# Attention probabilities copied by DMA and transposed in one pass between the score products

## What is computed

```python
def sliding_window_attention(q, k, v, q_norm_g, k_norm_g, sinks):
    # 16 query heads in 4 groups of 4, one key/value head per group, head width 64, blocks of 128 tokens
    def block(args):
        qn, kn, vn, n = args          # keys: 16 meta tokens, the block before, the own block
        scores = einsum('bqhgd,bkhd->bhgqk', qn, keys) - slopes * dist
        scores = where(valid, scores, -inf)
        m = maximum(max(scores), sink)
        p = exp(scores - m)
        probs = p / (sum(p) + exp(sink - m))
        return einsum('bhgqk,bkhd->bqhgd', probs, vals)
```

## Time and profile before

| | |
|---|---|
| time, median of three runs | 1619.56 us (1619.38 to 1620.76) |
| span of the profiled execution, first to last instruction | 1618.2 us |
| TensorE busy | 1610.1 us, 99% |
| VectorE, ScalarE, GpSimd busy | 64%, 48%, 27% |
| granted TensorE clock | 1.000 over the span |

### The profile page before, as it was taken

How to read it: one execution, slowest core, us unless ns; L and a number is a source line. 1 busy time by engine, 2 the same in 40 slices (tenths; PEclk the granted TensorE clock), 3 DMA queues, 4 the chain that set the end, 5 groups by cost and what they waited for, 6 DMA issues and landing times.

```text
span 1618.2 us, 22594 instructions
## 1 busy us (share of the span) xinstructions
PE 1610.1 (99%) x7984; PEld 1347.5 (83%) x7984; DVE 1030.6 (64%) x1913; ACT 769.9 (48%) x1567; POOL 437.1 (27%) x675
## 2 busy tenths in 40 slices
PE   9999999999999999999999999999999999999999
PEld 6888888888888888888888888888888888888887
DVE  6775556655657676757565338866665657766675
ACT  6533334545547676763222126655545544444442
POOL 1101010221359888875221000121111122100000
PEclk9999999999999999999999999999999999999999
DMA  8323232645424343438553223344444399733452
GB/s 289 116 98 117 95 124 72 232 166 186 162 88 114 84 94 83 106 82 262 164 202 104 72 65 124 129 170 150 149 144 148 119 321 356 239 98 98 149 183 92
DMA packets 119599, 236.53 MB, mean 146 GB/s; under 512 B 13904, under 2 KB 48128, under 8 KB 119488
## 3 DMA queue, kind: packets, MB, share of 16 engines
q0 software_dynamic: 45904, 126.93, 23.6%
q1 hardware_dynamic: 73440, 108.03, 21.6%
q10 hardware_dynamic: 144, 0.13, 0.0%
HBM read 157.05 MB, written 69.47 MB: 140 GB/s over the span
## 4 chain that ended last, share of the span: by engine, by line
PE 97%; DVE 1%; DMA 1%; ACT 0%; SPq 0%; POOL 0%; issue 0%; DVEq 0%; ACTq 0%
PE bank L1084 29%; PE bank L1089 29%; PE bank L1088 29%; PE bank L1370 2%; PE bank L1402 2%; PE bank L1384 2%; PE bank L1419 0%; PE bank L1127 0%; PE bank L1502 0%; PE bank L1288 0%; PE bank L1406 0%; PE bank L1452 0%; DMA PX<-in_w_in 0%; PE bank L1387 0%; DVE WL L2172 0%; PE bank L1427 0%
## 5 line engine op out<-in xcount | busy, mean ns | idle before, releaser
L1084 PE MATMUL bank<-WH,ADH 128*128 128x512 f32 x448 | 174.3, 389 | 0.0
L1088 PE MATMUL bank<-WH,ADL 128*128 128x512 f32 x448 | 174.3, 389 | 0.0
L1089 PE MATMUL bank<-WL,ADH 128*128 128x512 f32 x448 | 174.3, 389 | 0.0
L1084 PE MATMUL bank<-HN,WH 128*128 128x512 f32 x384 | 152.4, 397 | 0.0
L2098 ACT CAST ADH<-ARAW 128x512 fp32r<-128x512 f32 x112 | 69.5, 621 | 169.9 <-PE bank L1089 160.9
L1089 PE MATMUL bank<-HN,WH 128*128 128x512 f32 x384 | 150.3, 391 | 0.0
L1088 PE MATMUL bank<-HN,WL 128*128 128x512 f32 x384 | 150.0, 391 | 0.0
L959 POOL TENSOR_SCALAR PR<-PR,RC 128x272 f32<-128x272 f32 (+1 forms) x128 | 131.0, 1099 | 44.9 <-DVE RC L2663 44.4
L2917 DVE TENSOR_TENSOR ADL<-ARAW,ADH 128x512 fp32r<-128x512 f32 x112 | 77.5, 692 | 96.9 <-ACT ADH L2098 96.7
L1084 PE MATMUL bank<-SOPH,WH 128*128 128x512 f32 x256 | 99.8, 390 | 0.0
L1089 PE MATMUL bank<-SOPL,WH 128*128 128x512 f32 x256 | 99.6, 389 | 0.0
(11 more groups left out here) (356 smaller groups left out, 4242.8 us busy)
## 6 DMA issues: line engine op xcount, KB each, us to landing
ARAW<-uop SPq DMA_DIRECT2D x112, 256.0 KB, 3.0
uop<-US POOLq DMA_DIRECT2D x64, 256.0 KB, 2.8
WRAW<-in_w_up SPq DMA_DIRECT2D x15, 1024.0 KB, 6.2
RAW<-in_w_in SPq DMA_DIRECT2D x58, 256.0 KB, 4.0
gates<-TB POOLq DMA_DIRECT2D x48, 256.0 KB, 2.4
uop<-UA POOLq DMA_DIRECT2D x48, 256.0 KB, 3.1
proj<-SA POOLq DMA_DIRECT2D x36, 256.0 KB, 2.5
RT<-proj POOLq DMA_DIRECT2D x8, 1024.0 KB, 8.8
```

Source lines behind the costliest of these rows:

```text
L1084: mm = pe.matmul(bank, ahi, bhi, start=first, stop=False, skip_group_check=onto)
L1088: pe.matmul(bank, alo, bhi, start=False, stop=False, skip_group_check=onto)
L1089: return pe.matmul(bank, ahi, blo, start=False, stop=last, skip_group_check=onto)
```

## The change

The probabilities of a pair are copied by a DMA of SyncE's queue from `PR` (fp32) into a new tile `PW` of two slots, whose type is fp32r, and TensorE transposes them from there with the fp32r identity `IDR`, one pass each. The transposes belong to pair T-3 instead of T-2 (LAG = 3), so that the loop has 68 steps and all that follows the transposes (`take_p`, `lo_p`, `values`, the moves of outputs) comes one step later; `values` stand in odd steps now. The transposes are no longer one group ahead of the query and key transposes: they stand singly behind the score products. To make room for `PW`, the keys and values of the blocks (`KV`) lie in a ring of four (NKV) instead of eight places, with their loads on GpSimd moved to steps 20, 28, 36 and 44, and the two weight blocks that lay in free places of it have a place of their own (`RAWA`). `PR` is freed for the next scores by the copy's landing, not by the transposes. As 220 gate steps are now spread over 68 steps, `new_slabs` gives 2, 3, 3 blocks in steps 6 to 8, 3, 3, 2 in steps 26 to 28, and 4, 3, 1 in steps 46 to 48.

```diff
@@ constants
-STEPS = NPAIR + 3
+LAG = 3
+STEPS = NPAIR + LAG + 1
-KV_FREE = {4: (6, 7), 5: (0, 7), 6: (0, 1)}
+ASIDE = (4, 5, 6)
+
+NKV = 4
@@ sync: the loop
+            def copy_p(pair):
+
+                n, b = pair // 8, pair % 2
+                lo, hi = (0, 2 * NKEY) if n else (P, P + 2 * NKEY0)
+                sp.wait_ge(pn_rdy, pair + 1)
+                if pair >= 2:
+                    sp.wait_ge(pt_full, pair - 1)
+                sp.dma_start(PW[:, b, lo:hi].bitcast(F32), PR[:, pair % 3, 1 + lo:1 + hi]).then_inc(pw_full[b], 16)
+
             for T in range(STEPS):
+                if 2 <= T < NPAIR + 2:
+                    copy_p(T - 2)
...
-                if T >= 4 and T % 2 == 0:
-                    G = (T - 4) // 2
+                if T >= LAG + 2 and T % 2 == 1:
+                    G = (T - LAG - 2) // 2
@@ tensor: the loop
-            def transpose_p(pair):
-                n, b = pair // 8, pair % 3
-                pe.wait_ge(pn_rdy, pair + 1)
-                if pair >= 1:
-                    pe.wait_ge(pl_rdy, split_of(pair - 1))
...
+            def transpose_p(pair, c):
+                n, b = pair // 8, pair % 2
+                if c == 0:
+                    pe.wait_ge(pw_full[b], PW0 + 16 * (pair // 2 + 1))
+                    if pair >= 1:
+                        pe.wait_ge(pl_rdy, split_of(pair - 1))
...
+                elif c // 2 in slots_of(n):
+                    key = pr_slot(n, c % 2, c // 2) - 1
+                    pe.transpose(B[4][:, c * P:(c + 1) * P].bitcast(F32R), PW[:, b, key:key + P], IDR[:, :])
...
-                if T < NPAIR:
-                    scores(T)
+                for i in range(5):
+                    if T < NPAIR and i < 4:
+                        score(T, i)
+                    if LAG <= T < NPAIR + LAG:
+                        transpose_p(T - LAG, i)
@@ vector: top(T)
                 if T >= 3:
-                    dve.wait_ge(pt_full, T - 2)
+                    dve.wait_ge(pw_full[(T - 3) % 2], PW0 + 16 * ((T - 3) // 2 + 1))
```

More of the change, by code:

```diff
@@ L589, in raw_block @@
                 return RAW[:, place, :] if place < 4 else RAWE[place - 4][:, :]
-            if k in (4, 5) and slab in KV_FREE:
-                return KV[:, KV_FREE[slab][k - 4], :]
+            if k in (4, 5) and slab in ASIDE:
+                return RAWA[:, k - 4, :]
             return RAWE[k - 4][:, :] if k >= 4 and slab == SLAB_E and RA_E else RAW[:, raw_slot(slab, k), :]
@@ L1358, in _, with score @@
                     ahead[i]()
-            def scores(T):
-                n, p = T // 8, T % 8
+            def score(T, i):
+                n, p, hl, part = T // 8, T % 8, i // 2, i % 2
                 g = p // 2
-                if p % 2 == 0:
+                if p % 2 == 0 and i == 0:
                     pe.wait_ge(aqT_rdy, 4 if n == 0 else 4 * n + g + 1)
                     pe.wait_ge(akT_rdy, 4 if n == 0 else 4 * n + g + 1)
[L1366 to L1371, removed]
-                    mm.then_inc(sc_full, 1)
@@ L1374, in transpose_p @@
-            def transpose_p(pair):
-                n, b = pair // 8, pair % 3
-                pe.wait_ge(pn_rdy, pair + 1)
-                if pair >= 1:
-                    pe.wait_ge(pl_rdy, split_of(pair - 1))
[L1379 to L1385, removed]
-                    pe.wait_ge(pl_rdy, meta_of(pair // 2 - 1))
-                pe.transpose(B[6][:, (pair % 2) * P:(pair % 2 + 1) * P],
-                             PR[:, b, 1 + 2 * P:1 + 3 * P], IDN[:, :]).then_inc(pt_full, 1)
+                if T >= 1 and part == 0:
+                    pe.wait_ge(nm_rdy, 2 * (T - 1) + hl + 1)
@@ new lines, in score @@
+                mm = pe.matmul(B[2 + hl][:, 0:NKEY if n else NKEY0], QT[:, 2 * p + hl, :], KTS[:, part, g, keys_of(n, hl)],
+                               start=part == 0, stop=part == 1)
+                if part == 1:
+                    mm.then_inc(sc_full, 1)
+            def transpose_p(pair, c):
[4 more added lines that the diff above has]
+                        pe.wait_ge(pl_rdy, split_of(pair - 1))
+                    else:
+                        pe.wait_ge(aqT_rdy, 4)
+                if c == 4:
+                    if pair % 2 == 0 and pair >= 2:
+                        pe.wait_ge(pl_rdy, meta_of(pair // 2 - 1))
+                    pe.transpose(B[6][:, (pair % 2) * P:(pair % 2 + 1) * P].bitcast(F32R),
+                                 PW[:, b, 2 * P:3 * P], IDR[:, :]).then_inc(pt_full, 1)
+                elif c // 2 in slots_of(n):
+                    key = pr_slot(n, c % 2, c // 2) - 1
+                    pe.transpose(B[4][:, c * P:(c + 1) * P].bitcast(F32R), PW[:, b, key:key + P], IDR[:, :])
@@ L1433, in _ @@
                     gate_step(i)
-                if T >= 4 and T % 2 == 0:
-                    values((T - 4) // 2)
-                if 2 <= T < NPAIR + 2:
-                    transpose_p(T - 2)
+                if T >= LAG + 2 and T % 2 == 1:
+                    values((T - LAG - 2) // 2)
                 if T in NEXT_Q:
@@ L1941, in _ @@
                         g.then_inc(a_free if c < 16 else th_rdy, 1)
-                if 2 <= T < NPAIR + 2:
-                    take_p(T - 2)
-                if T >= 4 and T % 2 == 0:
-                    take_y((T - 4) // 2)
+                if LAG <= T < NPAIR + LAG:
+                    take_p(T - LAG)
+                if T >= LAG + 2 and T % 2 == 1:
+                    take_y((T - LAG - 2) // 2)
                 if T % 8 == 2 and T // 8 + 1 < NB:
@@ L2675, in _ @@
                         split_lo(slab, k)
-                if T > NPAIR:
+                if T > NPAIR + 1:
                     for slab, k in new_slabs(T):
                         split_lo(slab, k)
-                if T >= NPAIR and T < NPAIR + 2:
+                if NPAIR + 1 <= T < NPAIR + 3:
                     for b in range(4):
-                        lo_ys(4 * (T - NPAIR) + b, b, T - NPAIR)
-                splits = new_slabs(T) if T < NPAIR else []
+                        lo_ys(4 * (T - NPAIR - 1) + b, b, T - NPAIR - 1)
+                splits = new_slabs(T) if T <= NPAIR else []
                 if T % 8 == 0 and T // 8 + 1 < NB:
@@ L2695, in _ @@
                     lo_v(T // 8 + 1).then_inc(ql_rdy, 1)
-                if T != NPAIR:
+                if T != NPAIR + 1:
                     gated(T)
```

57 lines of the change are left out of this document (28 added, 29 removed).

## The result

The changed kernel takes 1642.21 us (median of 4 runs, 1640.66 to 1644.84), the kernel before beside it 1619.47 us (1619.09 to 1620.76). The ratio is 1.0138 with an interval of 1.0124 to 1.0153. So the change costs 22.7 us. The forecast was a loss of 7.1 us and a range that ended at 1632: the side was right, the size wrong by a factor of three. All of it arises in the attention loop: from the first score product to the end of the last `values` it is 266.2 us before and 288.4 with the change, and what follows takes 890.0 and 889.5.

What follows compares the result with a forecast made beforehand. It took TensorE, busy in 99% of the span, as the bound. Savings of 3.3 us, 9.9 for late copies and 0.5 for later transposes gave +7.1 on 1619.56: 1626.6 us, range 1617.5 to 1632.

Steps and rivals of the forecast that it cites:

- What it costs behind the weight loads: Steps 10, 28 and 48, with small waits after: TensorE waits for copies queued behind weight loads, 9.9 us (5.8 to 14).
- the 2.1 us for the transposes: Attention loop groups: one-pass transposes singly between scores save 2.1 us in all, bounds 1.1 and 3.2.
- The copy of pair T-2 is issued in SyncE's step T, behind all loads of step T-1: SyncE's queue: those loads wait for VectorE's splits, and TensorE transposes the pair in step T+1; waits of 9.9 us.
- two small ones: Steps 30 and 50: smaller waits for copies behind the loads of steps 28 and 48, 0.3 and 0.6 us.
- VectorE's delay: Attention loop: the last transpose comes 0.5 us later, 0.86 with query or key transposes, and everything on VectorE follows.
- I take a value between: Copy landing: about 3.0 us, between 64 KB output moves at 2.6 and 256 KB weight loads at 3.2.
- The last burst has no loads in this loop and costs nothing: Last burst of the attention loop: no waits for copies, cost nothing.
- 0.50 + 0.33 + 0.09 + 0.11 = 1.03: TensorE's group of nine: four scores, three transposes, the fourth, and the last take 1.03 us, against 1.05 before.
- hardly less than an fp32 one: One-pass transposes in a row on TensorE: 0.093 us each, against 0.11 for fp32.
- the 1.2 us: TensorE's three waits for GpSimd's normalised pair: the later step covers 1.2 us of 1.4, bounds 0.9 and 1.4.
- the faster rivals: Whole kernel: hidden weight loads 1615.3 us, chance 0.08; copies never late 1616.8, 0.10; late by half 1620 to 1621, 0.12.
- the one of slower landings: Whole kernel: scores wait in most odd steps, or DMA traffic slows landings everywhere; 1630 to 1636 us, chance 0.15.

Runs made afterwards that it cites:

- e1: The changed kernel with each copy issued one step earlier in SyncE's stream, ahead of that step's weight loads: 1622.62 us, ratio 1.0014.
- e4: The changed kernel with the four weight loads of step 60 put behind the copy of step 61: 1639.84 us, ratio 1.0122.
- e5: The changed kernel with 48 surplus products on TensorE during the waits of steps 10, 28, 48 and 62: 1639.56 us, ratio 1.0117.
- e9: The same kernel as e5, against the changed kernel, run once more for a profile: 1638.64 us, ratio 1.0116.

## Why the prediction was right in its side and wrong in its size

**The term that failed.** "What it costs behind the weight loads" stood at 9.9 us. By e1 the late copies cost about 20 us: 15.3 us of waits, since a landing close behind loads was priced too low and step 62 was left out, and some 4 to 6 us of slow clock behind them, which had no term. A smaller term failed beside it, the 2.1 us for the transposes.

**The place and the mechanism were right.** "The copy of pair T-2 is issued in SyncE's step T, behind all loads of step T-1": this is what the trace shows in steps 10, 28 and 48, and e1 takes it away with one line. TensorE waits there 3.2, 3.5 and 3.6 us, 10.3 in all, where 9.9 stood for these and two small ones. But the two parts of that term were off in opposite ways. The landings were 4.0, 4.5 and 5.0 us instead of 3.0, 4.5 us more in the sum, while TensorE needed the copies later than worked out: in step 48 one is issued 1.4 us ahead of the need (664.16, with the idle time beginning at 665.57), where the prediction had 0.4. VectorE's delay wasn't what was wrong. From the end of step 26's group to the end of its third split it is 573.50 - 567.59 = 5.91 us, and 569.12 - 564.23 = 4.89 before, so 1.0 later where 0.9 stood. But the working left out that the four query or key transposes now stand ahead of the first transpose in steps 10, 28 and 48, and that the first score of steps 28 and 48 waits for its maximum:

```profile
573.98 0.45 PE L1432 MATMUL bank<-IDR,QST 128*128 128x128 f32 x4
574.67 0.36 PE L1381 MATMUL bank<-KTS,QT 128*128 128x272 f32 x1 [0.24 <-DVE NM L2644]
```

That puts the need 0.7 us later in step 28 alone. That 10.3 came so close to the 9.9 is luck: two errors of more than 3 us nearly cancelled.

**The landing was taken from a row for another situation.** "I take a value between" 2.6 and 3.2 was good for the median (3.1), and the prediction named the effect in its upper bound, a landing a microsecond slower with a load in flight just ahead. At every place that counted, loads were in flight just ahead: that was the very reason why the copy was late. The bound should have been the estimate. The Trainium skill has a rule that bears on it, "DMA: Bandwidth & Descriptors", section Queues, rings and completion order: a DMA's semaphore increment is written only after every earlier write of the same DMA engine, so by it a copy that shares all its DMA engines with the loads ahead of it isn't seen to land before them. The trace agrees: in all four places the copy lands behind the last load, by 0.7 to 1.7 us. No run here separates this from plain sharing of the engines' bandwidth.

**"The last burst has no loads in this loop and costs nothing" was wrong.** It counted the loads that wait for splits, and overlooked the four loads of step 60, which need 2.2 us in the queue ahead of a copy, which then lands after 6.2. Step 62 waits 2.2 us; e4 shows the cause. Steps 8, 19 and 43 weren't worked out either, and step 9 had only a few tenths; the four have 2.8 us. All waits for copies are 15.3 instead of 9.9: 5.4 us more.

**The one-pass transposes save 0.3 us against the kernel before, not 2.1.** The step that failed is "0.50 + 0.33 + 0.09 + 0.11 = 1.03". A score with its transpose takes 717.13 - 716.89 = 0.24, where 0.125 + 0.11 = 0.235 stood. The term went wrong at the group's end: the start of the first gate product lies 0.97 behind the first score, which flatters it, and its weights come 0.08 later against its recorded start. And in a row, where the prediction had "hardly less than an fp32 one" at 0.093, they take 0.073 against 0.11. So its reading that the row offers nothing was wrong as well: the row is where the 5 to 6 us are.

**The clock wasn't in the sum at all.** The prediction took every wait at its length. Three of them were followed by stretches at half clock; up to 6.5 us by the windows, about 4 net by e5 and e9. TensorE's busy time says 5.7: 1616.8 us, and 1611.1 in e1, which has the same products at full clock. The Trainium skill warns of such waits, in "TensorE: Matmul & The Clock Gate", section Loop structure matters more than you think: an engine that sits idle for a long DMA wait comes back at the lower clock. The trace agrees for three of the four waits of 2.2 us and more, and not for the one of 3.2 in step 10. The prediction used that page for issue gaps and didn't ask it about the waits that it forecast.

**Right:** no wait for GpSimd is left, so the 1.2 us were covered. Waits of the scores for the maximum are 0.6 us beside 0.5. None of the faster rivals came true, and the one of slower landings came nearest.

The account on the span: 7.1 forecast, + 5.4 for the copies, + 0.1 for the scores, + 1.8 for the transposes, + 6.5 for the clock = 20.9, with 21.6 measured. That it closes within 0.7 is partly luck, as the clock's term is an upper bound. With the 4 net of e5 and e9 it stays some 3 us short, and e1 has a rest of about the same kind: 2.5 us over the kernel before, with neither long waits nor a slow clock. No run shows what makes up this rest.

## What to carry to other kernels

A transfer that the critical engine waits for must not stand in an in-order queue behind transfers that wait for slower work; where there is room, move it ahead by a step, and work out the rest after that. Price such a wait with the landing of a transfer that has others in flight ahead of it, not with the median, and add what a fall of the clock costs: here it fell behind most idle times of 2.2 to 4.0 us. Where one kind of product is changed for a shorter one, measure to the second product behind the group, and try it in a row with its like before putting it singly between longer ones.

## What the runs showed of the hardware that was not expected

- TensorE's clock fell to the 1.2 GHz level behind single idle times of 2.2 to 4.0 us, in a kernel that keeps TensorE busy for 99% of its time, and not behind all of them: 3.2 us in step 10 left it at 1.00, while 2.2 us in step 62 of the same execution brought it to 0.59.
- Surplus products in the idle time made the kernel faster: 48 of them kept the clock at 1.000 and took about 4 us off.
- A copy of 272 KB within SBUF lands after 3.1 us in the median, and after 6.2 behind four loads of 256 KB, 0.7 behind the last of them.
- A one-pass 128x128 transpose costs 0.073 us in a row with its like, where an fp32 one costs 0.11. Singly between score products of 272 columns it costs 0.11 as well, and a whole group with one-pass transposes is only 0.02 us shorter than one with fp32 transposes.
